# A two-layer block: fourteen conditioning vectors summed by VectorE behind the even mixer instead of by TensorE in it

## What is computed

```python
c_act = jax.nn.silu(c)
for layer in range(DEPTH):
    mod = c_act @ cond_w[layer] + cond_b[layer]
    sh_m, sc_m, g_m, sh_f, sc_f, g_f = [m[:, None, :] for m in jnp.split(mod, 6, axis=-1)]
    h = x * (1.0 + sc_m) + sh_m
    y = even_mixer(h, ...) if layer % 2 == 0 else retention_mixer(h, ...)
    x = layer_norm(ALPHA * x + g_m * y, ...)
    h = x * (1.0 + sc_f) + sh_f
    y = swiglu(h, ...) if layer % 2 == 0 else moe_swiglu(h, ...)
    x = layer_norm(ALPHA * x + g_f * y, ...)
```

## Time and profile before

| what | value |
|---|---|
| median of 3 runs | 1742.43 us (1740.64 to 1743.49) |
| profiled execution | 1742.85 us |
| its span | 1740.9 us |
| TensorE busy | 1617.3 us (93%) |
| VectorE busy | 1282.3 us (74%) |
| ScalarE busy | 1009.3 us (58%) |
| mean granted TensorE clock | 0.966 |

### The profile page before, as it was taken

How to read it: one execution, slowest core, us unless ns; L and a number is a source line. 1 busy time by engine, 2 the same in 40 slices (tenths; PEclk the granted TensorE clock), 3 DMA queues, 4 the chain that set the end, 5 groups by cost and what they waited for, 6 DMA issues and landing times.

```text
span 1740.9 us, 20082 instructions
## 1 busy us (share of the span) xinstructions
PE 1617.3 (93%) x7810; PEld 1297.4 (75%) x7810; DVE 1282.3 (74%) x1160; ACT 1009.3 (58%) x867; POOL 132.8 (8%) x94
## 2 busy tenths in 40 slices
PE   4888996999969999879999999999999999999996
PEld 1874765787858777658888888888888888888875
DVE  1374536655456665688889888898898898988986
ACT  1432223444434444347777777777777777777775
POOL 0421310000000100220000000000000000000005
PEclk8898998999989999979999999999999999999998
DMA  9347885855454543539999999999999999999993
GB/s 329 130 167 283 322 316 193 285 183 185 169 169 146 164 171 145 187 129 391 388 379 390 375 388 387 369 388 379 376 389 375 381 388 371 384 385 367 385 382 151
DMA packets 234370, 515.33 MB, mean 296 GB/s; under 512 B 8936, under 2 KB 40960, under 8 KB 234176
## 3 DMA queue, kind: packets, MB, share of 16 engines
q1 hardware_dynamic: 228272, 491.99, 77.3%
q10 hardware_dynamic: 2992, 11.79, 1.9%
q0 software_dynamic: 3008, 10.20, 1.9%
HBM read 507.15 MB, written 13.11 MB: 299 GB/s over the span
## 4 chain that ended last, share of the span: by engine, by line
PE 86%; DVE 7%; issue 2%; ACT 2%; DMA 2%; POOL 1%; DVEq 0%; SPq 0%; ACTq 0%; POOLq 0%
PE bank L762 25%; PE bank L764 25%; PE bank L763 25%; PE bank L741 2%; PE bank L925 2%; DMA ring<-in_cond_w 2%; PE bank L1185 1%; PE bank L757 1%; DVE arena L1768 1%; DVE small L1689 1%; PE bank L774 0%; ACT w_part L1310 0%; DVE w_part L1643 0%; DVE hs L1715 0%; PE bank L1167 0%
## 5 line engine op out<-in xcount | busy, mean ns | idle before, releaser
L1654 DVE TENSOR_TENSOR w_lo<-ring,w_hi 128x2048 fp32r<-128x2048 f32 x336 | 764.7, 2290 | 104.1 <-ACT w_hi L1537 102.2
L1537 ACT ACTIVATE w_hi<-ring 128x2048 fp32r<-128x2048 f32 x334 | 640.5, 1918 | 196.3 <-PE bank L764 187.0
L762 PE MATMUL bank<-w_lo,heT_hi 128*128 128x512 f32 x896 | 353.8, 395 | 3.8 <-DVE w_lo L1654 2.2
L764 PE MATMUL bank<-w_hi,heT_hi 128*128 128x512 f32 x896 | 349.7, 390 | 0.0
L763 PE MATMUL bank<-w_hi,heT_lo 128*128 128x512 f32 x896 | 348.9, 389 | 0.0
L1643 DVE TENSOR_TENSOR w_part<-ring,w_part 128x1024 fp32r<-128x1024 f32 x148 | 183.4, 1246 | 211.0 <-ACT w_part L1310 206.2
L1310 ACT ACTIVATE w_part<-ring 128x1024 fp32r<-128x1024 f32 (+1 forms) x162 | 169.1, 1049 | 252.0 <-PE bank L764 247.3
L762 PEld LDWEIGHTS bank<-w_lo,heT_hi 128*128 128x128 f32 x896 | 168.3, 188 | 39.0 <-issue 5.9
L764 PEld LDWEIGHTS bank<-w_hi,heT_hi 128*128 128x128 f32 x896 | 168.2, 188 | 35.9
L763 PEld LDWEIGHTS bank<-w_hi,heT_lo 128*128 128x128 f32 x896 | 168.5, 188 | 33.6
L762 PE MATMUL bank<-w_part,hT_hi 128*128 128x512 f32 (+1 forms) x448 | 179.8, 401 | 14.2 <-DVE w_part L1643 13.1
(11 more groups left out here) (344 smaller groups left out, 1586.8 us busy)
## 6 DMA issues: line engine op xcount, KB each, us to landing
ring<-in_moe_w_up SPq DMA_DIRECT2D x224, 1024.0 KB, 8.8
ring<-in_moe_w_down SPq DMA_DIRECT2D x112, 1024.0 KB, 7.8
ring<-in_cond_w SPq DMA_DIRECT2D x24, 2048.0 KB, 9.1
ring<-in_ffn_w_up SPq DMA_DIRECT2D x22, 1024.0 KB, 8.2
ring<-in_od_w_in SPq DMA_DIRECT2D x8, 2048.0 KB, 7.9
ring<-in_ev_w_in SPq DMA_DIRECT2D x5, 2048.0 KB, 12.4
ring<-in_ffn_w_down SPq DMA_DIRECT2D x5, 2048.0 KB, 7.7
ring<-in_od_w_in SPq DMA_DIRECT2D x8, 1024.0 KB, 8.0
```

The source lines that it names most:

```text
L762: mm(bank, lhs[0], rhs[1], start=start, stop=False)
L764: return mm(bank, lhs[0], rhs[0], start=False, stop=stop)
L1537: f(w_hi[:, n % 3], half_landed(act, it, u, half), ACT.Copy) \
L1654: tt(w_lo[:, buf], at, w_hi[:, buf].bitcast(F32), ALU.subtract).then_inc(S["w_lo"], 1)
```

## The change

Ten vectors stay as they were, in two batches: the first four, and (0, 4) to (0, 9). The other fourteen, (0, 10), (0, 11) and all of layer 1 (`SUM_COND`), are no longer multiplied by PE. Their loads move in the list of units: one behind every second unit, from ffn_up 1 to od_g 3 (`SUM_AT`). VectorE sums them in `sum_cond`: one scaling of a bias row set (`sum_bias`, loaded by GpSimd at the start, and a column of the unit matrix that picks the row), then for each of the eight chunks a multiply-add of the 128x512 weights with a column of c, into `acc`. `split_to` calls it behind each part's remainder, for one step, and for two behind a unit's last part (and behind both parts of ffn_down 5); it takes no step for a vector whose load stands behind the part's unit in the list. The last step raises `summed`, on which `slot_read` now makes SP wait, and PE too: `cond` for these is one product of a matrix of ones with `acc`. The spreading is moved to `SPREAD_AT`, behind later units; the last two stand behind the router. The thirteen calls of `cond_rows` from the key and query products of the even mixer onward go, with the third batch's bias products and copy. Banks are shared by eight from the second batch on. At the end, VectorE does the last norm's weights for both tiles. The descriptor scratch of software DMAs is set to 4096, which makes room for `sum_bias`.

```diff
+COND_BATCHES = (tuple((0, u) for u in FIRST_COND), tuple((0, u) for u in range(4, 10)))
+SUM_COND = ((0, 10), (0, 11)) + tuple((1, u) for u in range(N_COND))
...
-UP_COND = {0: (0, 10), 1: (0, 11), 2: (1, 0), 3: (1, 1), 4: (1, 2), 5: (1, 3), 6: (1, 4), 7: (1, 5), 8: (1, 6), 9: (1, 7)}
-DOWN_COND = {0: (1, 8), 2: (1, 9)}
-OD_COND = {0: 10, 1: 11}
+SUM_AT = {
+    ("ffn_up", 1): 0, ("ffn_up", 3): 1, ("ffn_up", 5): 2, ("ffn_up", 7): 3, ("ffn_up", 9): 4,
+    ("ffn_down", 0): 5, ("ffn_down", 2): 6, ("ffn_down", 4): 7,
+    ("od_v", 0): 8, ("od_qk", 1): 9, ("od_g", 1): 10, ("od_v", 2): 11, ("od_qk", 3): 12, ("od_g", 3): 13,
+}
+SPREAD_AT = {
+    ("ffn_up", 4): (0,), ("ffn_up", 6): (1,), ("ffn_up", 8): (2,), ("ffn_up", 10): (3,),
+    ("ffn_down", 2): (4,), ("ffn_down", 4): (5,),
+    ("od_qk", 0): (6,), ("od_g", 0): (7,), ("od_v", 1): (8,), ("od_qk", 2): (9,), ("od_g", 2): (10,), ("od_v", 3): (11,),
+    ("router",): (12, 13),
+}
...
-    order = c(0, *FIRST_COND) + e(0, 1, 2, 5, 4, 3) + c(0, *range(4, N_COND)) + c(1, *range(N_COND))
+    order = c(0, *FIRST_COND) + e(0, 1, 2, 5, 4, 3) + c(0, *range(4, 10))
...
+    for key, n in SUM_AT.items():
+        order.insert(order.index(key) + 1, ("cond", *SUM_COND[n]))
     return order
...
-            if key[0] == "cond":
+            if key[0] == "cond" and key[1:] in SUM_COND:
+                eng.wait_ge(S["summed"], SUM_COND.index(key[1:]) + 1)
+            elif key[0] == "cond":
                 eng.wait_ge(S["cond_used"], cond_order.index(key[1:]) + 1)
...
+                if (l, u) in SUM_COND:
+                    n = SUM_COND.index((l, u))
+                    pe.wait_ge(S["summed"], n + 1)
+                    mm(bank[:], ones, acc[:, n % 2], start=True, stop=True).then_inc(full, 1)
+                    return
...
                        ALU.subtract).then_inc(S["w_lo"], 1)
+                    sum_cond(key, 2 if key[-1] == 3 or key[:-1] == ("ffn_down", 5) else 1)
...
+            def sum_cond(key, steps):
+
+                for _ in range(steps):
+                    n, k = sums[0] // (KC + 1), sums[0] % (KC + 1) - 1
+                    if n == len(SUM_COND) or stream_place["cond", *SUM_COND[n]] > stream_place[key[:-1]]:
+                        return
+                    sums[0] += 1
+                    l, u = SUM_COND[n]
+                    total = acc[:, n % 2]
+                    if k < 0:
+                        filled(dve, "cond", *(SUM_COND[n - 2] if n > 1 else (0, 9)))
+                        dve.wait_ge(S["sum_bias_in"], 16)
+                        col = N_COND * l + u
+                        V.do(ts(total, sum_bias[:], ident[:, col:col + 1], None, ALU.mult))
+                        continue
+                    _, w = weights(dve, "cond", l, u)
+                    V.wait()
+                    last = stt(total, w[:, 512 * k:512 * k + 512], cT[:, k:k + 1], total, ALU.mult, ALU.add)
+                    if k < KC - 1:
+                        V.do(last)
+                    else:
+                        last.then_inc(S["summed"], 1)
...
+            affine(3, 0)
             affine(3, 1)
...
-            pool.wait_ge(S["ln_in"], 32 * 4)
-            pool.wait_ge(S["normed"], 3 * NT + 1)
-            G.then(tt(xs[:, 0], xs[:, 0], ln[:, 0], ALU.mult))
-            tt(xs[:, 0], xs[:, 0], ln[:, 1], ALU.add).then_inc(S["first_done"], 1)
```

More of the change, by code:

```diff
@@ L183, in pe_order @@
         o += ([("ws", n)] if n else []) + ([("kv", n)] if n < 3 else [])
-    o += [("go", t) for t in range(NT)] + [("cond_rows", 2)]
+    o += [("go", t) for t in range(NT)]
     o += [("hT", 1, i) for i in (2, 3, 0, 1)]
@@ L188, in pe_order @@
     for u in range(FFN // 256):
-        o += [("ffn_up", u, t) for t in range(NT)] + ([("cond", *UP_COND[u - 1])] if u - 1 in UP_COND else [])
+        o += [("ffn_up", u, t) for t in range(NT)] + [("cond", *k) for k in spread_at("ffn_up", u)]
         o += [("ffn_T", u - 1)] if u else []
     o += [("ffn_down", t, h) for t in range(NT) for h in range(2)] + [("ffn_T", FFN // 256 - 1)]
-    o += [("cond", *key) for key in DOWN_COND.values()]
+    o += [("cond", *k) for i in range(6) for k in spread_at("ffn_down", i)]
     o += [("hT", 3, i) for i in BY_TILE]
     for h in range(RH):
-        o += [("od_qk", h, t) for t in range(NT)]
+        o += [("od_qk", h, t) for t in range(NT)] + [("cond", *k) for k in spread_at("od_qk", h)]
         if h:
-            o += [("cond", 1, OD_COND[h - 1])] if h - 1 in OD_COND else []
             o += [("ret_y", h - 1, t) for t in range(NT)]
-        o += [("od_v", h, t) for t in range(NT)] + [("ret_T", h, t) for t in range(NT)]
-        o += [("od_g", h, t) for t in range(NT)] + [("ret_s", h)]
+        o += [("od_v", h, t) for t in range(NT)] + [("cond", *k) for k in spread_at("od_v", h)]
+        o += [("ret_T", h, t) for t in range(NT)]
+        o += [("od_g", h, t) for t in range(NT)] + [("cond", *k) for k in spread_at("od_g", h)] + [("ret_s", h)]
         if h:
@@ L205, in pe_order @@
     o += [("hT", 4, i) for i in BY_TILE]
-    o += [("routerT",), ("router",), ("rank",)]
+    o += [("routerT",), ("router",)] + [("cond", *k) for k in spread_at("router")] + [("rank",)]
     o += [("rows_T", 0), ("rows_T", 1)]
@@ L758, in cond, with spread @@
                     .then_inc(full, 1)
+            def spread(*key):
+                for l, u in spread_at(*key):
+                    cond(l, u)
             def three(bank, lhs, rhs, start, stop):
@@ L1082, in ffn_between @@
                     ffn_turn(FFN // 256 - 1)
[L1083 to L1084 removed]
+                spread("ffn_down", i)
                 taken(pe, "ffn_T", min(2 * i + 1, FFN // 256 - 1))
@@ L1454, in _ @@
             for i in range(6):
-                if i > 1 and i - 2 in DOWN_COND:
-                    cond(*DOWN_COND[i - 2])
+                spread("ffn_down", i)
                 split_ahead("ffn_down", i)
```

53 lines of the change are left out of this document (27 added, 26 removed).

## The result

| | before | after |
|---|---|---|
| time, median (range), us | 1742.96 (1740.64 to 1743.52) | 1931.57 (1929.68 to 1933.24) |
| profiled span, us | 1740.9 | 1931.0 |
| PE busy | 93% | 85% |
| mean granted clock of TensorE | 0.966 | 0.915 |

The ratio is 1.1085, with an interval of 1.1065 to 1.1104: 188.6 us slower. The forecast was 1900, with a range of 1845 to 1940.

The account below looks back on a forecast made before the run. The prediction took TensorE (PE), busy 93% of the span, as the bound. Its terms, -18.5 + 2 + 133.9 + 10.7 + 30 - 0.6 = +157.5 us on the profiled 1742.85, gave 1900 us, range 1845 to 1940.

Parts of the forecast that it names:

- The likeliest case: Whole kernel: the load stalls occur but their sizes are off, 1900 us, some 1865 to 1930; chance 0.82.
- the moved spreading: Fourteen one-row products on PE stay fourteen, the last two going behind the router where PE waits for VectorE: 0.
- The stalls: Feed-forward and odd mixer: loads queued behind SP's wait for a sum stall PE, 133.9 us at fourteen places, plus 10.7.
- The clock: Behind each of 15 PE gaps the clock falls to half, 2.0 us lost each: +30 us, bounds 15 and 46.
- The even mixer: Fourteen vectors' row products, 1.85 us each, leave PE in the even mixer: -18.5 us, bounds 26 and 12 gained.
- VectorE's sums: Steps fit VectorE's gaps in the feed-forward, cost 0.7 us three times in the odd mixer: +2, bounds 0 and 84.
- The fifteenth place: At ffn_up 2, whose load shares the DMA engines with ScalarE's slots-table fill: +10.7 us, bounds 5 and 12.
- The tail: At the end, the first tile's affine moves from GpSimd to VectorE: -0.6 us, bounds -1 and +1.
- Router and experts: Two late vectors behind the router and the smaller descriptor scratch: 0, or +11 us if indirect reads waited for each other.
- That the loads keep up: Rival: queued units land in time in feed-forward and odd mixer, leaving only the gain, 1723 us; chance 0.07.
- that VectorE's time is paid: Rival: no load is late, but all of VectorE's sums lie on the path, 1807 us; chance 0.06.
- that queued units land together: Rival: queued loads share the DMA engines, the wanted unit landing up to 5.4 us later at 12 places, 1965 us; chance 0.05.

Follow-up runs that it names:

- without loads: The changed kernel without the fourteen moved vectors' loads, VectorE summing the bias tile instead, so those vectors are not computed: 1868.53 us, ratio 1.0725.
- other steps: The changed kernel with three sum steps behind a unit's last part and two behind each other part (1784.38 us), or three and one (1847.69 us).
- constant products in the waits: The changed kernel with five products of constants ahead of PE's waits between the even mixer's states: 1927.28 us, ratio 1.1060.
- steps 3 and 1: The changed kernel with three sum steps instead of two behind a unit's last part, still one behind other parts: 1847.69 us, ratio 1.0604.
- the copies early: The changed kernel with sum steps three and two, and ScalarE's six slots-table copies issued in the even mixer, not the feed-forward: 1773.09 us, ratio 1.0178.

## Why the prediction was right, and where its sizes were off

The likeliest case is what happened, by its own mechanism; the sum of +157.5 became +190.1 in the profiled execution. The time lies in the range, but above the 1930 that the prediction names as the top of this case. Its own bounds add up to more: 1900 + 14 + 16 + 6.5 = 1936.5. Nearly every term came out dearer than forecast; only the moved spreading went clearly the other way. Term by term:

- **The stalls, 144.6 forecast, 155.4 measured.** Right at every place, and within 0.7 us at ten of the fifteen; the four ffn_up places of 11.3 each came to 43.9 against 45.1. Mis-sized are od_v 1 (11.72 against 8.0), where the unit took 16.3 us from its issue to landing and not 12.9, od_out 2 (7.49 against 4.4), where the landing was 9.45 and not 7.9, and od_out 0 (10.89 against 8.5) and ffn_down 3 and 5 (1.4 and 1.3 more), which weren't taken apart. The release of 2.4 to 3.1 us, the landing of 12.8 for a unit behind a vector and the 2.5 for rounding and splitting are all in the chain above. The experiments without loads and with other steps show the cause, the chain only the path.
- **The clock, 30 forecast, 38.6 measured.** The prediction took 2.0 us for each gap. After and the kernel without loads give PE the same work in these stages, so PE's busy time tells the clock's share: in the feed-forward 215.9 against 194.6 us, 21.3 more or 2.7 for each of its 8 gaps; in the odd mixer 229.1 against 211.8, 17.3 more or 2.5 for each of 7. The stages add up with it: +103.7 are 86.5 of stalls, -5.2 of spreading, 1.1 for VectorE and 21.3; +95.6 are 68.9, 3.4, 4.9 for VectorE, 1.1 for the short waits (the three of after against 2.75, 1.89 and 2.75 without loads, with some smaller ones) and 17.3. The windows behind the gap at 370.7 show it directly:

```profile
370.60:372.60 2.00, 1.92 (x5) 1.57 (x6) 2.00 (x4) 1.49 (x4) 0.00 (x0) 0.50 1.10 349
...
374.60:376.60 2.00, 2.00 (x6) 1.56 (x5) 1.08 (x3) 0.43 (x1) 0.00 (x0) 0.50 0.00 0
376.60:378.60 2.00, 2.00 (x9) 1.60 (x9) 1.33 (x2) 0.63 (x1) 0.00 (x0) 0.94 0.00 0
```

  It is half, the 1.2 GHz level, for about six us behind this gap: 3 lost. Behind the gap at ffn_up 2 it is 0.50 from 334.6 to 338.6 and 0.83 in the two us behind. Of the two rows at hand the prediction took a middle; the nearer one was that of 108 to 110 us, which gives 3. Together it is 2.0% of the span. The Trainium skill, TensorE: Matmul & The Clock Gate, Part 1, puts the ramp under 1% of a typical span, in a passage on the first products of a kernel; here it is paid behind fifteen gaps, and the prediction was right to count gaps. The section of the Trainium skill "Loop structure matters more than you think", on products that wait for a DMA each time, agrees with this trace: half clock behind every one of the fifteen.
- **The even mixer, -18.5 forecast, -10.1 measured.** This is the step that failed, though it is the smaller part of what the forecast missed. All its prices were right for a PE at full clock. The prediction counted the row products as mere work in PE's way and did not ask what PE would be without them: a PE with small products and waits for VectorE. The clock fell to 0.72 and 0.83, and the products that remain were slower. PE's timeline in after:

```profile
234.96 2.05 PE L1028 MATMUL bank<-arena 128*128 128x128 f32 x8 [1.26 <-issue]
```

  The same eight products take 1.16 us in before. With the constant products in the waits 5.4 of the 8.4 us come back, so most of the difference is shown to be the clock's. The other 3 are the clock's too, at another place: behind the key and query products, where a row product went as well. After and the kernel with steps 3 and 1 have the same instructions there and the same wait of 2.07 us, but not the same clock behind it. After first, then the other:

```profile
175.53 1.11 PE L930 MATMUL bank<-cst,arena 128*128 128x128 f32 x4 [2.07 <-DVE arena L1910]
```

```profile
174.62 0.66 PE L930 MATMUL bank<-cst,arena 128*128 128x128 f32 x4 [2.07 <-DVE arena L1910]
```

  The clock is 0.50 behind the wait in after for about six us, and 1.00 in the other. From the wait at 160 us to the feed-forward it is 138.3 us in after, and 135.0 in the kernel without loads and in both kernels with other steps, whose clock stayed up there too: 13.5 less than in before, not 10.3. The profiles with the copies early and with constants have the low clock, as after. So kernels that are the same up to there differ by some 3 us, and a comparison of two profiles can't be read finer than that.
- **VectorE's sums, +2 forecast, +6 measured** (1.1 and 4.9, by the kernel without loads). Near the low end, as argued: the gaps of 1.5 us beside each part hold the step. In the odd mixer the short waits behind rotation and head norm cost twice what was put down.
- **The fifteenth place, 10.7 forecast, 11.34 measured,** and gone with the copies moved. Where the prediction had nothing for the moved spreading, it was -5.2 and +3.4.
- **The tail, -0.6 forecast, -0.8 measured.** From the start of the last bn_stats to the end of VectorE's work it is 7.05 us against 7.85. As forecast, shift and multiplication run at their usual pace without GpSimd beside them, 0.16 and 1.22 us for 1.02 and 2.12; VectorE's timeline in after:

```profile
1922.96 0.16 DVE L1749 SCALAR_TENSOR_TENSOR small<-small 128x1 f32<-128x1 f32 x1
...
1925.45 1.22 DVE L1756 TENSOR_TENSOR xs<-xs,ln 128x1024 f32<-128x1024 f32 x1
```

- **Router and experts** were forecast at 0. From the router to the end it is +1.0 with the tail's -0.8 in it, so +1.8, the descriptor scratch and the two late vectors among it; it wasn't taken apart.
- **The rivals.** That the loads keep up is refuted by SP's rows; that VectorE's time is paid, by the kernel without loads; that queued units land together, by the times to landing: at the ffn_up places the vector lands in 7.8 to 8.1 us and the wanted unit behind it in 12.4 to 12.8, and only at od_v 1 is it 11.3 and 16.3, which wasn't taken apart.

In sum the differences are +10.8 for the stalls, +8.6 for the clock behind them, +8.4 in the even mixer, +4 for VectorE, +1.1 for the short waits, -1.8 for the spreading, and +1.6 from the router to the end: 32.7, against 190.1 - 157.5 = 32.6.

## What to carry to other kernels

Where one queue loads a ring in order, work out for each load when the slot it takes was released, and count as late everything behind it in the queue: a slow reader of one slot stops loads that have a free one. A sum that is spread thinly beside other work must end before its slot's turn comes, and one step more in the right place was worth 84 us here; nine sums with three units each, in place of fourteen with two, turned the loss into a gain of 9, and of 15 with the loads one unit sooner and the copies spread over the levels. Before work is taken out of an engine's way, look at what remains between its waits: small work in the gaps may be what keeps its clock up. Before a few microseconds are put down to an edit, look at the same stretch in kernels that don't differ there.

## What the runs showed of the hardware

- Behind a gap of about 11 us TensorE's granted clock is half for some five to six us, and a gap of 7.5 to 12.7 us costs 2.6 us of slower products in the mean. Behind short gaps it varies: behind one of 3.52 us it was 0.50 and then 0.67, behind one of 3.25 us it stayed at 1.00, and behind the same wait of 2.07 us in the same instructions it was 0.50 in three kernels' profiles and 1.00 in three others'. A stretch of small products that wait for VectorE had 1.00 with row products among them, 0.72 without, and 0.90 with products of constants.
- Six copies from DRAM to DRAM hold up weight loads beside them: 17.4 to 22.4 us to landing, against 5.3 to 9.3. Moved ahead of the weights' stretch they brought 11.3 us; in a kernel whose loads stand there they cost 14.
- The issue of such copies is not free for the engine that issues them: 0.61 to 1.63 us each on ScalarE, in the way of what stands behind.
